# When two expert weight parts are loaded: tables moved in on-chip memory, and the load order of the mixture-of-experts stage's first slots

## The chip, the cores and the metric

The kernel runs on one core of a Trainium2 chip. Times are device microseconds of one launch. The kernel before took 649.22 us, the median of three runs (646.59, 649.22, 649.32).

## The reference, cut to what matters

One step of a one-layer decoder on 544 tokens (512 of a prompt, 32 of 8 samples), width 1024, all in float32:

```
xn     = rms_norm(x); u, v, xr, g_a, g_b = split(xn @ w_in)        # 1024 x 5120
merged = sigmoid(g_a) * (gelu(u) * spatial_gating(layer_norm(gelu(v)))) + sigmoid(g_b) * rg_lru(conv(xr))
x1     = x + merged @ w_out                                         # 1024 x 1024
xf     = rms_norm(x1)
group  = argmax(xf @ w_rg + b_rg)          # of 4; softmax value pg
e1, e2 = top2 of the group's 8 experts     # softmax values pe, renormalised
y      = sum over e1, e2 of gate * ((silu(xf @ w_gate[e]) * (xf @ w_up[e])) @ w_down[e])
out    = rms_norm(x1 + y)
```

There are 32 experts, each with 3 MB of weights (`w_gate`, `w_up` 1024 x 256, `w_down` 256 x 1024), so that about 100 MB must come from memory whatever the tokens choose.

## The kernel before, in words

The first part (to about 300 us of the span) normalises the tokens and computes the input projection, the spatial gating and the recurrent branch, channel block by channel block. The output projection follows: 16 units (numbers 40 to 55, `STEPS` is 56), eight for token group A (tiles 0, 1 and the samples' tile 4), eight for group B (tiles 2, 3). Each unit's weights go through one of four `raw` buffers. Beside the units of group B, VectorE already routes group A. When the last unit is done (`unit_done` = `STEPS`), group B is routed: a rank of every token within its expert, then one-hot tables `posh`, `toks` and `rsk`, from which TensorE makes two tables, first the token indices (`idx`, released by `tab_ready`), then the row scales `rt` (released by `rt_mm`).

The expert stage handles experts in pairs, 64 tokens each, side by side on the 128 partitions. There are 16 pairs and, with these inputs, one further single expert that has more than 64 tokens. For each pair GpSimd gathers 128 token rows from the buffer `xnd` in device memory into `xg` (semaphore `xg_in`), TensorE transposes them (L1817), multiplies by gate and up weights (L1829), transposes the product (L1842), multiplies by the down weights (L1855), and GpSimd scatters the rows to `ytok`. At the end the rows come back (`gy`), are weighted, added to the residual and normalised.

Weights live in six slots of 24 KB a partition, `wslot[q][s]` with q = 0, 1, 2 and s = 0, 1; pair G uses q = G mod 3. Each expert comes in three parts of 1 MB: part 0 (first half of gate and up), part 1 (second half), part 2 (down). All of them are issued by SyncE, in program order, in one queue. SyncE's program around the change: the units' loads `step_in(n)`; experts 0 and 1 have long been in slots (0,0) and (0,1); the loop over n = 48 to 55 also issues the three parts of expert 4 into slot (2,0); then `row_out(p, count)` writes the finished residual tiles to `xnd`, each waiting for VectorE's `x1_ready`; then comes the wait for the last unit, the rest of the six slots, and `refill` for all later pairs, which waits for TensorE to be done with a part (`gu_half`, `gu_mm`, `pair_mm`) before it issues the next one into it.

On-chip memory is laid out by hand, and the six slots overlap with things of the earlier stages. Slot (2,1) covers 72 to 96 KB, of which 72 to 80 KB is the projection's third split buffer, and the rest was free early. Slot (1,1) covers 122 to 146 KB, of which the last 16 KB is `raw`; the routing tables (`R_T`) stood at 138 KB, in its part 2. `dgs` (two diagonal matrices of gates) is made by VectorE after `rt` and announced by `dgs_ready`.

The semaphore names of the prediction: `dgs_ready` (L1336), `rt_mm` (L1790), `xg_in` (L635), `tab_ready` (L1321), `x1_ready` (L1143). SyncE's lines: L467 issues a part of an expert in the opening, L489 a unit, L500 a residual tile, L537 and L553 a refill, L570 the last pair's parts, L581 the final reads.

Of the kernel before, what the change touches and what calls it, by code (L numbers as in the profile page):

```python
# [22 lines left out]
P = 128  # L23
D = 1024
# [4 lines left out]
S = DB * DS  # L29
TA = SEQ + S  # L30
TILES = NT + 1
# [21 lines left out]
GROUP_A, GROUP_B = (0, 3), (3, 5)  # L53
# [55 lines left out]
def build(nc, x, wmix, wgate, chan, wst, bs, rows, wr, br, wmoe, y, vp, vs, st):  # L109
# [3 lines left out]
    def at(name, offset, shape, dt=F32):  # L113
        return nc.alloc_sbuf_tensor_at(name, shape, dt, offset=BASE + offset)

    K = 1024
# [2 lines left out]
    GU = KT * 512  # L119
    EW = GU + 2 * D  # L120
    wslot = [[at(f"wslot{q}{s}", (first + s * 24) * K, [P, EW]) for s in range(2)]
             for q, first in enumerate((0, 98, 48))]
    xh = at("xh", 48 * K, [P, KT, SEQ], F32R)
    xl = at("xl", 64 * K, [P, KT, SEQ], F32R)
    zT = at("zT", 80 * K, [P, KT, TA])

    R_V = 162 * K
    v = at("v", 0, [P, TILES, D])
    x1 = at("x1", R_V, [P, TILES, D])
    tw = TA * 4  # L130
    XRW = 3 + SEQ + DB * 7
    (XC, A, TR, TI, M, U, U1, GA) = [at(n, R_V + i * tw, [P, TA]) for i, n in
                                     enumerate(("xc", "a", "tr", "ti", "m", "u", "u1", "ga"))]
    XR = at("xr", R_V + 8 * tw, [P, XRW])

    R_M = 98 * K
    mh = at("mh", R_M, [P, KT, SEQ], F32R)
    ml = at("ml", R_M + 16 * K, [P, KT, SEQ], F32R)
    xt = at("xt", R_M, [P, TILES, D])
    lng = at("lng", R_M + 20 * K, [P, D])  # L140
    lnb = at("lnb", R_M + 24 * K, [P, D])
    g1r = at("g1r", 80 * K, [P, D])
    junk = at("junk", R_M + 28 * K, [P, D])
    bterm = at("bterm", R_M + 28 * K, [P, KT, P])
    vo = at("vo", R_M, [P, 2, D])

    R_W = 130 * K
    raw = at("raw", R_W, [P, RAW, KT, P])
    wh = at("wh", R_W + 16 * K, [P, 2, D], F32R)
    wl = at("wl", R_W + 24 * K, [P, 2, D], F32R)  # L150

    wh2 = at("wh2", 72 * K, [P, D], F32R)
    wl2 = at("wl2", 76 * K, [P, D], F32R)
    R_T = R_W + 8 * K
    posh = at("posh", R_T, [P, 2, TILES, P], BF16)
    colh = at("colh", R_T + 2560, [P, 2, TILES, PAIRS], BF16)
    toks = at("toks", R_T + 2880, [P, 2, 2, TILES, 2, PAIRS], BF16)
    pick = at("pick", R_T + 4160, [P, 2, TILES, NE])
    rsk = at("rsk", R_T + 5440, [P, 3, 2, TILES, PAIRS], BF16)
    junk2 = at("junk2", 96 * K, [P, 512])  # L160
    yf = at("yf", 122 * K, [P, TILES, D])

    gy = at("gy", 48 * K, [P, 2, TILES, D])
    nf = at("nf", 88 * K, [P, D])
# [1 line left out]

    R_E = R_W + 16 * K
    xg = at("xg", R_E, [P, D])
# [3 lines left out]
    hm = at("hm", R_E + 13 * K, [P, FE])  # L172
    hT = at("hT", R_E + 14 * K, [P, 2, P])

    top = [182 * K]

    def small(name, shape, dt=F32):
        size = 4
        for n in shape[1:]:
            size *= n  # L180
        t = at(name, top[0], shape, dt)
        top[0] += -(-size // 32) * 32
        return t
# [1 line left out]
    ch = small("ch", [P, KT, NCH])  # L185
    ident = small("ident", [P, P])
    ones = small("ones", [P, P], F32)
    upper_at = top[0]
    upper = small("upper", [P, P], F32)
    fold = small("fold", [P, S])  # L190
    late = top[0]
# [47 lines left out]
    first = small("first", [P, NE])  # L239
# [3 lines left out]
    gate = small("gate", [P, 2, TILES])  # L243
    T2 = 2 * TILES
    rk = small("rk", [P, 2, TILES])
    (rkx, chk, bx, posx) = [at(n, upper_at + 256 + i * 64, [P, T2]) for i, n in enumerate(("rkx", "chk", "bx", "posx"))]
    caps = small("caps", [P, MAXCHUNK - 1])
    xcnt = small("xcnt", [P, 3, NE])
    cnt17 = small("cnt17", [1, EXTRA])
# [9 lines left out]
    warm = small("warm", [P, 1])  # L259
    turn = small("turn", [P, 4])  # L260
    eps = small("eps", [P, 1])
    dgs = at("dgs", upper_at, [S, 2, S])
    WH, WL = (wh[:, 0, :], wh[:, 1, :], wh2[:]), (wl[:, 0, :], wl[:, 1, :], wl2[:])
    assert BASE + top[0] <= nc.sbuf_usable_end, top[0] / K

    with ExitStack() as ctx:
        ps = ctx.enter_context(nc.psum_tensor("ps", [P, 8, 512], F32))

        def sem(name):
            return ctx.enter_context(nc.semaphore(name))  # L270
# [13 lines left out]
        xg_in = sem("xg_in")  # L284
# [95 lines left out]
        dgs_ready = sem("dgs_ready")  # L380
# [6 lines left out]
        def rowsof(t):  # L387
            return S if t == NT else P
# [38 lines left out]
        def _(sp_):  # L427
            e = sp_
# [30 lines left out]
            def expert(q, s, n):  # L459

                for part in range(3):
                    expert_part(q, s, n, part)

            def expert_part(q, s, n, part):

                lo, hi = PARTS[part]
                e.dma_start(wslot[q][s][:, lo:hi], wmoe[n][:, lo:hi]).then_inc(part_in[part][q][s], 16)  # L467
# [16 lines left out]
            def step_in(n):  # L484

                e.wait_ge(lo_ready, n - 3)
                if n < O_FIRST + UNITS_O + RAW:
                    e.wait_ge(rows_mm, UNITS_V // 2 + (1, 1, 2, 3, 2, 3, 4, 4)[n - O_FIRST - RAW])
                e.dma_start(raw[:, n % RAW, :, :], wmix[unit_at(n)]).then_inc(raw_in[n % RAW], 16)  # L489
# [6 lines left out]
            def row_out(p, count):  # L496

                t = TILE_AT[p]
                e.wait_ge(x1_ready, count)
                e.dma_start(xnd[t * P:t * P + rowsof(t), :], x1[0:rowsof(t), t, :]).then_inc(xn_stored, 16)  # L500
# [9 lines left out]
                residual_in(p)  # L510
            for n in range(48, STEPS):
                step_in(n)
                if n % 2 and n < 54:
                    expert_part(2, 0, 4, (n - 49) // 2)
            expert_part(2, 1, 5, 1)
            expert_part(2, 1, 5, 2)
            for p in range(*GROUP_A):
                row_out(p, 4 + p)
            row_out(3, 9)
            row_out(4, 10)  # L520
            e.wait_ge(unit_done, STEPS)
            expert(1, 0, 2)
            expert_part(1, 1, 3, 0)
            e.wait_ge(dgs_ready, 2)
            expert_part(1, 1, 3, 1)
            e.wait_ge(rt_mm, 1)
            expert_part(1, 1, 3, 2)
            expert_part(2, 1, 5, 0)

            def refill(q, count, number):  # L530

# [944 lines left out]
        def _(pe):  # L1476
# [48 lines left out]
            def nothing(*_):  # L1525
                pass
# [444 lines left out]
```

## Time and profile before

| | us |
|---|---|
| median of three runs | 649.22 |
| the profiled execution | 649.22 |
| its span in the profile | 647.5 |
| TensorE busy | 599.0 |
| VectorE busy | 322.7 |
| ScalarE busy | 229.3 |
| GpSimd busy | 52.4 |

The span is the time from the first to the last recorded instruction; 1.7 us of the execution lie outside it. The mean of TensorE's granted clock was 0.97 of full speed. All parts of the expert weights, 97 transfers of 1024 KB and four of 512 KB, are issued by SyncE; the page's line of GB/s shows how the transfers are spread over the span. A matmul here streams 512 columns of float32.

### The profile page before, as it was taken

How to read it: one execution, taken by the hardware profiler on the slowest of the kernel's cores; microseconds unless marked ns; L12 is line 12 of the kernel's file. 1: busy time of each engine (PE TensorE's matmuls, PEld its weight loads, DVE VectorE, ACT ScalarE, POOL GpSimd, SP SyncE). 2: the span in 40 equal slices, each digit the busy share in tenths (PEclk: the TensorE clock that was granted, in tenths of full speed). 3: DMA queues.
4: the chain of work that ended last, by engine and by line, in shares of the span. 5: the costliest groups of instructions: out<-in, count | busy, mean ns of one | idle time of the engine just before them, and what ended most of it. 6: DMA issues, size and time to landing. Idle time of an engine off the chain costs nothing.

```text
span 647.5 us, 8845 instructions
## 1 busy us (share of the span) xinstructions
PE 599.0 (93%) x2860; PEld 359.8 (56%) x2860; DVE 322.7 (50%) x672; ACT 229.3 (35%) x393; POOL 52.4 (8%) x126
## 2 busy tenths in 40 slices
PE   6899999999999999999999978999999988987794
PEld 3676697877778777787578733433333333332320
DVE  4834698857767677685664855111001102100058
ACT  5423425474564745647263311111111111111124
POOL 1200001000000000000000021112121221111000
PEclk9899999999999999999997969999999999999996
DMA  8421316731222312222596389999999999999993
GB/s 308 163 86 66 126 37 240 329 106 65 73 73 97 105 65 73 73 98 71 200 412 274 134 325 414 417 420 420 419 420 421 421 419 420 420 418 419 416 320 138
DMA packets 33448, 160.61 MB, mean 248 GB/s; under 512 B 6320, under 2 KB 6704, under 8 KB 21008
## 3 DMA queue, kind: packets, MB, share of 16 engines
q1 hardware_dynamic: 27808, 149.52, 58.6%
q0 software_dynamic: 5472, 10.63, 4.5%
q8 instruction: 14, 0.23, 0.1%
q10 hardware_dynamic: 144, 0.15, 0.1%
q14 instruction: 10, 0.08, 0.0%
HBM read 155.01 MB, written 14.17 MB: 261 GB/s over the span
## 4 chain that ended last, share of the span: by engine, by line
PE 65%; SPq 12%; DMA 9%; DVE 8%; ACT 3%; issue 2%; ACTq 0%; DVEq 0%; POOLq 0%
PE ps L1486 14%; PE ps L1487 13%; PE ps L1488 13%; SPq L537 11%; PE ps L1829 8%; DMA wslot<-in_wmoe 5%; PE ps L1855 5%; PE ps L1605 2%; PE ps L1637 2%; DMA gy<-ytok 2%; PE ps L1691 1%; DMA ytok<-yo,idx 1%; PE ps L1589 1%; PE ps L1495 1%; PE ps L1628 1%
## 5 line engine op out<-in xcount | busy, mean ns | idle before, releaser
L1829 PE MATMUL ps<-wslot,xgT 128*64 128x512 f32 x528 | 121.7, 594 | 11.6 <-DMA wslot<-in_wmoe 10.2
L699 ACT ACTIVATE wh<-raw 128x1024 fp32r<-128x1024 f32 x56 | 59.1, 1058 | 153.5 <-PE ps L1488 138.1
L1486 PE MATMUL ps<-xh,wh 128*128 128x512 f32 x256 | 102.5, 401 | 0.0
L1488 PE MATMUL ps<-xl,wh 128*128 128x512 f32 x256 | 100.0, 390 | 0.0
L1487 PE MATMUL ps<-xh,wl 128*128 128x512 f32 x256 | 99.9, 390 | 0.0
L908 DVE TENSOR_TENSOR wl<-raw,wh 128x1024 fp32r<-128x1024 f32 x56 | 68.5, 1223 | 45.9 <-ACT wh L699 44.9
L1829 PEld LDWEIGHTS ps<-wslot,xgT 128*64 128x64 f32 x528 | 40.0, 137 | 88.5 <-issue 86.6
L1855 PE MATMUL ps<-wslot,hT 128*64 128x512 f32 x264 | 62.1, 599 | 8.2 <-ACT hT L869 8.2
L1402 DVE SCALAR_TENSOR_TENSOR hm<-ps,rt,hs 128x256 f32<-128x256 f32 x12 | 5.8, 484 | 120.6 <-ACT hs L867 120.6
L1486 PEld LDWEIGHTS ps<-xh,wh 128*128 128x128 f32 x256 | 48.1, 188 | 16.1 <-issue 6.7
L1488 PEld LDWEIGHTS ps<-xl,wh 128*128 128x128 f32 x256 | 48.1, 188 | 10.5
L1487 PEld LDWEIGHTS ps<-xh,wl 128*128 128x128 f32 x256 | 48.2, 188 | 9.3
L1855 PEld LDWEIGHTS ps<-wslot,hT 128*64 128x64 f32 x264 | 18.5, 137 | 40.9 <-issue 28.7
L872 ACT ACTIVATE yo<-ps 128x1024 f32<-128x1024 f32 x17 | 17.4, 1023 | 65.4 <-PE ps L1855 65.4
L867 ACT ACTIVATE hs<-ps,rt 128x256 f32<-128x256 f32 x12 | 5.7, 474 | 82.0 <-PE ps L1829 82.0
L1402 DVE SCALAR_TENSOR_TENSOR hm<-ps,rtx,hs 128x256 f32<-128x256 f32 x5 | 2.4, 484 | 57.8 <-ACT hs L867 57.8
L1486 PE MATMUL ps<-wh,xh 128*128 128x512 f32 x64 | 26.8, 418 | 3.1 <-DVE xs L934 2.1
L1486 PE MATMUL ps<-wh,mh 128*128 128x512 f32 x64 | 27.2, 425 | 0.0
L1488 PE MATMUL ps<-wl,xh 128*128 128x512 f32 x64 | 25.9, 405 | 0.0
L1487 PE MATMUL ps<-wh,xl 128*128 128x512 f32 x64 | 25.9, 405 | 0.0
L1487 PE MATMUL ps<-wh,ml 128*128 128x512 f32 x64 | 25.9, 405 | 0.0
L1488 PE MATMUL ps<-wl,mh 128*128 128x512 f32 x64 | 25.8, 402 | 0.0
(331 smaller groups left out, 798.6 us busy)
## 6 DMA issues: line engine op xcount, KB each, us to landing
wslot<-in_wmoe SPq DMA_DIRECT2D x97, 1024.0 KB, 22.2
raw<-in_wmix SPq DMA_DIRECT2D x56, 512.0 KB, 4.1
gy<-ytok SPq DMA_DIRECT2D x8, 512.0 KB, 8.7
xt<-in_x SPq DMA_DIRECT2D x4, 512.0 KB, 7.0
x<-in_x SPq DMA_DIRECT2D x4, 512.0 KB, 4.5
xnd<-x SPq DMA_DIRECT2D x4, 512.0 KB, 8.0
wslot<-in_wmoe SPq DMA_DIRECT2D x4, 512.0 KB, 27.0
out_y<-yf SPq DMA_DIRECT2D x4, 512.0 KB, 2.7
```

The costliest lines, as they stand in the source:

```text
L537: e.dma_start(wslot[q][s][:, lo:hi], wmoe[bass.ds(number + s, 1), :, lo:hi].rearrange("a p c -> (a p) c")).then_inc(part_in[part][q][s], 16)
L699: a.activation(WH[hslot], raw[:, slot, :, :].rearrange("p k c -> p (k c)"), ACT.Copy).then_inc(hi_ready, 1)
L872: a.activation(yo[:], ps[:, 6:8, :].rearrange("p b c -> p (b c)"), ACT.Copy).then_inc(yo_sb, 1)
L908: d.tensor_tensor(WL[hslot], raw[:, slot, :, :].rearrange("p k c -> p (k c)"), WH[hslot].bitcast(F32), ALU.subtract).then_inc(lo_ready, 1)
L1402: d.scalar_tensor_tensor(out=hm[:], in0=ps[:, 2, FE:2 * FE], scalar=scale, in1=hs[:], op0=ALU.mult, op1=ALU.mult).then_inc(hm_ready, 1)
L1486: pe.matmul(out, sh, mh_, start=start, stop=False)
L1487: pe.matmul(out, sl, mh_, start=False, stop=False)
L1488: return pe.matmul(out, sh, ml_, start=False, stop=stop)
L1605: i = pe.matmul(ps[S * q:S * q + S, 6, :].rearrange("p (u c) -> p u c", u=4), xs[:, k, :], raw[:, :, k, :], start=k < 4, stop=k >= 4, tile ...
L1637: pe.matmul(ps[:, 4 + w, :], gw[:, w, :], XC[:, 0:SEQ], start=True, stop=True)
L1829: l = pe.matmul(ps[CAP * s:CAP * s + CAP, 2, :], xgT[:, c, CAP * s:CAP * s + CAP], wslot[q][s][:, c * 512:(c + 1) * 512], start=c == 0, st ...
L1855: l = pe.matmul(ps[CAP * s:CAP * s + CAP, 6 + h, :], hT[:, f, CAP * s:CAP * s + CAP], wslot[q][s][:, o:o + 512], start=f == 0, stop=f == 1 ...
```

## The change

Everything from 98 KB to 182 KB moves down by 1 KB, so that the small tiles have 1 KB more; `rkx`, `chk`, `bx`, `posx` and `dgs`, which shared the bytes of `upper`, get bytes of their own. The routing tables (`R_T`) move from 138 KB to 80 KB, and the scratch tile `junk2` from 96 KB to 88 KB: both now lie in parts 1 and 2 of slot (2,1), and part 2 of slot (1,1) is clear of them. SyncE's order follows:

- Parts 1 and 2 of slot (2,1) (expert 5) are no longer issued ahead of the residual tiles but, with part 0, after the wait for `rt_mm`.
- The wait for `dgs_ready` in front of part 1 of slot (1,1) (expert 3) becomes a wait for the first gather, `xg_in` at 16; part 2 of that slot follows at once and no longer stands behind `rt_mm`.
- The residual tiles of group A are issued inside the loop, after the last unit's load; their order to it is as before.

```diff
     wslot = [[at(f"wslot{q}{s}", (first + s * 24) * K, [P, EW]) for s in range(2)]
-             for q, first in enumerate((0, 98, 48))]
+             for q, first in enumerate((0, 97, 48))]
...
-    R_V = 162 * K
+    R_V = 161 * K
...
-    R_M = 98 * K
+    R_M = 97 * K
...
-    R_W = 130 * K
+    R_W = 129 * K
...
-    R_T = R_W + 8 * K
+    R_T = 80 * K
...
-    junk2 = at("junk2", 96 * K, [P, 512])
-    yf = at("yf", 122 * K, [P, TILES, D])
+    junk2 = at("junk2", R_T + 8 * K, [P, 512])
+    yf = at("yf", 121 * K, [P, TILES, D])
...
-    top = [182 * K]
+    top = [181 * K]
...
-    (rkx, chk, bx, posx) = [at(n, upper_at + 256 + i * 64, [P, T2]) for i, n in enumerate(("rkx", "chk", "bx", "posx"))]
+    (rkx, chk, bx, posx) = [small(n, [P, T2]) for n in ("rkx", "chk", "bx", "posx")]
...
-    dgs = at("dgs", upper_at, [S, 2, S])
+    dgs = small("dgs", [S, 2, S])
...
             for n in range(48, STEPS):
                 step_in(n)
-                if n % 2 and n < 54:
-                    expert_part(2, 0, 4, (n - 49) // 2)
-            expert_part(2, 1, 5, 1)
-            expert_part(2, 1, 5, 2)
-            for p in range(*GROUP_A):
-                row_out(p, 4 + p)
+                if n % 2:
+                    if n < 54:
+                        expert_part(2, 0, 4, (n - 49) // 2)
+                    else:
+                        for p in range(*GROUP_A):
+                            row_out(p, 4 + p)
             row_out(3, 9)
             row_out(4, 10)
             e.wait_ge(unit_done, STEPS)
             expert(1, 0, 2)
             expert_part(1, 1, 3, 0)
-            e.wait_ge(dgs_ready, 2)
+            e.wait_ge(xg_in, 16)
             expert_part(1, 1, 3, 1)
+            expert_part(1, 1, 3, 2)
             e.wait_ge(rt_mm, 1)
-            expert_part(1, 1, 3, 2)
-            expert_part(2, 1, 5, 0)
+            expert(2, 1, 5)
```

## Rows read from the trace of the kernel before

**Rows 1.** the page: GB/s in 40 slices; chain by engine; DMA issues
```profile
GB/s 308 163 86 66 126 37 240 329 106 65 73 73 97 105 65 73 73 98 71 200 412 274 134 325 414 417 420 420 419 420 421 421 419 420 420 418 419 416 320 138
...
PE 65%; SPq 12%; DMA 9%; DVE 8%; ACT 3%; issue 2%; ACTq 0%; DVEq 0%; POOLq 0%
...
wslot<-in_wmoe SPq DMA_DIRECT2D x97, 1024.0 KB, 22.2
```

**Rows 2.** windows of the expert stage: busy us per engine, PEclk, DMA share, GB/s
```profile
384.00:396.00 12.00, 10.06 (x49) 4.58 (x47) 9.34 (x28) 0.47 (x1) 1.49 (x3) 0.92 0.98 384
392.00:480.00 88.00, 81.60 (x438) 31.16 (x436) 16.34 (x32) 12.69 (x26) 16.42 (x26) 1.00 1.02 418
480.00:595.00 115.00, 101.92 (x468) 38.36 (x464) 16.32 (x28) 16.99 (x34) 20.56 (x34) 1.00 1.02 420
```

**Rows 3.** timeline of TensorE, experts' gate/up matmuls: start, us, what, [idle before]
```profile
505.36 7.04 PE L1829 MATMUL ps<-wslot,xgT 128*64 128x512 f32 x32
...
518.08 7.04 PE L1829 MATMUL ps<-wslot,xgT 128*64 128x512 f32 x32
...
532.88 3.65 PE L1829 MATMUL ps<-wslot,xgT 128*64 128x512 f32 x16 [1.86 <-DMA wslot<-in_wmoe]
...
548.84 7.08 PE L1829 MATMUL ps<-wslot,xgT 128*64 128x512 f32 x16
...
589.92 3.65 PE L1829 MATMUL ps<-wslot,xgT 128*64 128x512 f32 x16 [1.40 <-DMA wslot<-in_wmoe]
595.69 3.65 PE L1829 MATMUL ps<-wslot,xgT 128*64 128x512 f32 x16 [2.11 <-DMA wslot<-in_wmoe]
```

**Rows 4.** chain of waits at the end: start us, us, what
```profile
564.90 30.65 DMA wslot<-in_wmoe
...
607.23 8.14 DMA ytok<-yo,idx
```

**Rows 5.** timeline of SyncE's queue: start us, us, what it issued
```profile
337.96 0.91 SPq L467 DMA_DIRECT2D wslot<-in_wmoe  x2
338.92 26.76 SPq L500 DMA_DIRECT2D xnd<-x  x4
...
367.11 3.06 SPq L467 DMA_DIRECT2D wslot<-in_wmoe  x4
...
383.23 1.28 SPq L467 DMA_DIRECT2D wslot<-in_wmoe  x3
...
391.29 0.88 SPq L537 DMA_DIRECT2D wslot<-in_wmoe  x2
```

**Rows 6.** windows around the output projection's second half
```profile
338.00:350.00 12.00, 12.00 (x73) 10.06 (x73) 2.58 (x9) 2.93 (x5) 0.00 (x0) 0.72 1.02 414
351.00:366.00 15.00, 15.00 (x80) 12.71 (x80) 12.66 (x42) 4.55 (x8) 0.00 (x0) 1.00 0.01 4
```

**Rows 7.** what SyncE's queue waited for: us, times, longest
```profile
SPq L467 <- DVE dgs L1336: 13.0, 1, 13.0
```

**Rows 8.** timeline of all engines, gather, tables and gates
```profile
378.67 1.10 POOL L632 DMA_INDIRECT xg<-xnd,idx  x1 [109.30 <-DVE idx L1320]
...
379.11 1.38 PE L1788 MATMUL ps<-rsk,posh 128*128 128x16 bf16 x30
...
382.83 0.37 DVE L1336 TENSOR_SCALAR dgs<-ident,gate 32x32 f32<-32x32 f32 x2
383.47 0.18 PEld L1817 LDWEIGHTS ps<-ident,xg 128*128 128x128 f32 x1 [0.80 <-DMA xg<-xnd,idx]
```

**Rows 9.** windows of the gap before the stream
```profile
379.50:383.00 3.50, 3.50 (x32) 2.06 (x32) 1.30 (x9) 0.20 (x1) 1.30 (x2) 0.50 0.59 194
383.00:384.00 1.00, 1.00 (x2) 0.18 (x1) 0.21 (x2) 0.00 (x0) 0.00 (x0) 0.50 0.05 21
```

**Rows 10.** timeline of TensorE, the second and third pair
```profile
401.46 7.04 PE L1829 MATMUL ps<-wslot,xgT 128*64 128x512 f32 x32
...
416.27 4.08 PE L1829 MATMUL ps<-wslot,xgT 128*64 128x512 f32 x18
```

More of the change, by code:

```diff
@@ L187, in build @@
     ones = small("ones", [P, P], F32)
-    upper_at = top[0]
     upper = small("upper", [P, P], F32)
```

## The prediction

> **What bounds the kernel now.** The page comes first. Its line of GB/s shows two kinds of stretches: loads well under 330 through most of the first half, then a plateau of 414 to 421 from slice 25 to slice 38, that is from about 389 us to 615 us [rows 1]. The chain that ended last puts 65% on TensorE and 12% and 9% on SyncE's queue and on transfers [rows 1], but these are shares of the whole span, and the plateau has to be read by itself. The windows of that stage show the 16 DMA engines busy all the time (share 1.02) at 418 and 420 GB/s, with TensorE busy for 81.6 of 88 us and for 101.9 of 115 us [rows 2]. So transfers run flat out from the start of the stage; TensorE is served from filled slots at first and has caught up with the loads later. The timeline shows when: up to 518.08 us the pairs follow each other every 12.72 us without a wait; from 532.88 us on, gate and up matmuls begin after waits on `wslot` (1.86, 1.40 and 2.11 us in the three rows that show one, of five in all) [rows 3]. The last such wait sets the end. The chain goes through a weight transfer to 595.55 us (564.90 + 30.65), then one pair's matmuls, its scatter (8.14 us) and the final reads behind that [rows 4]. After 595.55 us, 51.95 us remain to the end of the span at 647.5 us, and nothing in them is touched by the change.
>
> The end is thus the start of the stream, plus all bytes that must follow, over 420 GB/s, plus a fixed tail. What counts about a part is whether it goes before the stream's start, in time in which the DMA engines have nothing else to do, or into the stream.
>
> **Two parts lose their free place.** Before, parts 1 and 2 of slot (2,1) are issued at 337.96 us, ahead of the residual tiles [rows 5]. The DMA engines are then busy until about 350 us (share 1.02), and idle for the 15 us from 351 to 366 us, at 4 GB/s [rows 6]. The two parts cost nothing there: without them the same stretch is idle for 20 us. After, they stand behind `rt_mm`, in the stream. Each is 1024 KB [rows 1], both are 2.10 MB, and at the 420 GB/s of rows 2 they take 4.99 us. The bounds are 4.9 us by 430 GB/s, a little over the plateau's fastest slice, and 5.5 us by the 384 GB/s of the stream's first 12 us, where it is still starting [rows 2]. I take 5.0, since the queue is never empty later, so that the bytes are paid for at the plateau's rate.
>
> The Trainium skill's "DMA: Bandwidth & Descriptors", section "Where 436 GB/s comes from", says that for loads from device memory the memory's side binds, at about 358 GB/s. By it the two parts would cost 5.9 us (an estimate from that page's figure) and the time would be 655.3 us. The plateau of 420 GB/s on this core disagrees, and the measurement decides.
>
> **The stream's restart.** Four parts are issued at 367.11 us in both kernels [rows 5]. Then SyncE waits. Before, it waits 13.0 us for `dgs` [rows 7] and issues the next three parts at 383.23 us [rows 5], just after VectorE's two `dgs` operations end at 383.20 [rows 8]. After, it waits for the first gather. GpSimd issues that at 378.67 us, once the index table is there, and TensorE, which waits for the same semaphore `xg_in`, begins to load the first gathered rows at 383.47 us, after 0.80 us of idle time put down to that gather [rows 8]. So `dgs_ready` goes and `xg_in` is late next, 0.2 us later: I take a restart at 383.45. Its early bound is the end of the gather's issue, 379.77 us, a gain of 3.5 us (nothing excludes that the semaphore came before TensorE looked); its late bound is 384.2, a cost of 1.0. For the value near `xg_in` = 383.4 speaks the window ahead of it: 194 GB/s of gather and scatter traffic from 379.5 to 383 us and only 21 in the next [rows 9], which is how the end of a gather and a scatter looks.
>
> Behind the new wait stand five parts and then every refill; nothing else is in SyncE's queue until the end. The `rt_mm` wait behind it costs nothing: that matmul group ends at 380.49 us (379.11 + 1.38) [rows 8], before the gather lands. Issuing goes at 0.43 us each (three in 1.28 us), so the five are out by 385.6 us, ahead of the first refill, which TensorE releases at 391.29 us [rows 5].
>
> **What depends on the delayed parts.** Parts 1 and 2 of slot (1,1) land some 5 us after the restart, at 389 us; the second pair needs them at 401.46 us. Slot (2,1), three parts, follows by about 396 to 398 us (5.24 MB at 420 GB/s from 383.5, plus gather traffic); the third pair needs them at 416.27 us [rows 10]. Both are covered, with 12 and 18 us to spare, so no pair stalls early. The refills queue behind 2.1 MB more and land 5 us later each; up to the eleventh pair this only eats the lead of the filled slots.
>
> **Edits without a cost.** The addresses change no instruction: the same forms on other offsets; `rkx` to `dgs` only get bytes of their own. If offsets mattered to VectorE's speed, its few dozen small operations of 0.2 us could shift by tenths of a microsecond; below that I have no row, and take 0 (from -0.2 to +0.2). The residual tiles of group A go out 0.9 us earlier (337.96 rather than 338.92 [rows 5]) and land about 5 us earlier, with the 2 MB gone from in front. Nobody waits for them: the first gather had been waiting for the index table [rows 8], and the last tile goes out in both cases just before 367.11. Gain 0.
>
> **Sum.** Profiled execution 649.22 us (span 647.5, 1.72 around it, and equal to the median shown). 649.22 + 4.99 + 0.22 = 654.4 us.
>
> **Rivals.** *TensorE's chain sets the end and the transfers are hidden.* For it: TensorE is busy for 93% of 392 to 480 us. Its point of decision is whether the weights' landings still have 5 us to spare at the last pairs. Then only the restart of the loads moves, nobody waits for it, and the time stays at 649.2 to 649.4 us, not slower. Against it: the waits of rows 3, from 532 us on, the last of them on the chain. Chance 0.08.
>
> *The gather lands well before TensorE looks.* The stream then restarts 2 to 3.5 us earlier, and the time is 650.9 to 652.4 us, middle 651.7. For it: TensorE was in filler matmuls around 383 us. Against it: the traffic of rows 9. Chance 0.09.
>
> *The projection gets its clock back.* Over 338 to 350 us TensorE's granted clock was 0.72 in the mean, while the DMA engines were saturated, and 1.00 from 351 to 366 us, when they were idle [rows 6]. If the 2 MB of traffic are the cause, 12 us at 0.72 shrink by 3.4, and everything behind comes as much earlier: 651.0 us. Against it: the router's short matmuls stand in this stretch, and the same DMA share beside the experts' matmuls goes with a clock of 1.00 [rows 2]. Chance 0.04.
>
> *Longer waits cost the clock.* With the loads 5 us later TensorE waits in more pairs. If a wait took it down to the 1.2 GHz level, the 7.3 us of matmuls of the chain after the last landing (3.65 of gate and up [rows 3], and as many of the same width for down) would double: 654.4 + 7.3 = 661.7 us. Against it: granted clock 1.00 over 480 to 595 us with waits of up to 2.11 us [rows 2, 3]. For it: 0.50 from 379.5 to 384 us, after a stretch of small matmuls and gaps [rows 9]. Chance 0.04. The Trainium skill's "TensorE: Matmul & The Clock Gate", section "HAM oscillation — how this bites in real kernels", says that a wait for a transfer between groups of matmuls sends the array back to its slow clock, group after group. By that rule the time is this rival's; the 1.00 in rows with such waits does not bear it out so far.
>
> **From the cases to the numbers.** The forecast has 0.75, and its own range is 653.2 to 655.8 us. The rest is 0.08, 0.09, 0.04, 0.04. Below 0.5% (3.2 us, the least that a measurement of this kernel can tell from no change) lie the first rival and most of the second and third, 0.08 + 0.07 + 0.03 = 0.18; one of the three runs before was 2.6 us below the others, so 0.02 of it goes to faster and 0.02 more of the forecast's goes to the same. That makes faster 0.02, same 0.18, slower 0.80. The range runs from 651.2 to 656.4: it takes in both ends of the transfer's price, the late restart, and the upper part of the early ones.
>
> **What would show it.** In the profile after: no weight parts between 338 and 366 us, and an idle DMA stretch of about 20 us that begins near 345. SyncE's wait ahead of L467 put down to the gather's `xg`, ending 0.2 us behind where the `dgs` wait ended, then five parts in a row. The pairs start at the same times up to about 500 us, with no wait at the second and third pair. The share stays at 1.02 and the rate at 420 GB/s. A pair takes 15.96 us once TensorE has caught up (from 532.88 to 548.84) against 12.72 before [rows 3], a loss of 3.2 us each, so its first wait on `wslot` comes one or two pairs earlier, around 505 to 520 us. The last landing in the chain moves from 595.5 to about 600.8 us, with the same 52 us behind it. The prediction falls if that landing moves by less than 2 us, if the restart is not at 383.2 to 384 us, or if a pair before the tenth waits for its weights.

## The result, and the profile after

The changed kernel takes 653.44 us, the median of nine runs, against 649.01 us of nine runs of the kernel before beside it. The ratio is 1.0066 (95% interval 1.0048 to 1.0085), that is 3.1 to 5.5 us slower. One of the nine took 865.06 us, in a slow state with a granted clock of 0.65 in the mean, and the ratio leaves it out. A second set of six runs gave 653.43 against 648.56 us and a ratio of 1.0070 (1.0050 to 1.0091). The ratios and their intervals are estimates from single runs and need not be the quotient of two medians. The profiled execution took 652.5 us, its span 650.9 us; before it was 649.22 and 647.5.

The page of the changed kernel, with the same two lines as in [rows 1]:

```profile
GB/s 309 159 87 66 128 34 257 310 106 73 68 68 97 105 73 73 64 107 86 217 407 103 220 331 421 419 420 419 417 422 420 420 419 421 419 419 420 413 315 137
...
PE 62%; SPq 16%; DMA 9%; DVE 8%; ACT 3%; issue 2%; ACTq 0%; DVEq 0%; POOLq 0%
```

In slices 21 to 23 (325 to 374 us) 407, 103 and 220 GB/s stand where the kernel before has 412, 274 and 134. Traffic is gone from slice 22, in the idle stretch, and the later stages' plateau of 413 to 422 runs as before. The windows that answer to [rows 2, 6] (columns as there):

```profile
338.00:350.00 12.00, 12.00 (x81) 10.16 (x80) 3.98 (x18) 2.93 (x5) 0.00 (x0) 0.86 0.70 254
392.00:480.00 88.00, 81.67 (x438) 31.42 (x438) 14.16 (x24) 13.81 (x28) 15.86 (x27) 1.00 1.02 420
480.00:595.00 115.00, 98.59 (x450) 37.73 (x448) 16.31 (x28) 15.88 (x32) 20.30 (x33) 1.00 1.02 420
```

The share stays 1.02 and the rate 420 GB/s. TensorE is busy for 98.6 us instead of 101.9 between 480 and 595 us, so it waits more. SyncE's queue, as in [rows 5]:

```profile
337.82 1.38 SPq L499 DMA_DIRECT2D xnd<-x  x3
...
365.33 3.06 SPq L466 DMA_DIRECT2D wslot<-in_wmoe  x4
...
381.57 2.58 SPq L466 DMA_DIRECT2D wslot<-in_wmoe  x5
...
388.95 4.26 SPq L536 DMA_DIRECT2D wslot<-in_wmoe  x4
```

The residual tiles come at 337.82 us with nothing in front of them, and the five parts in a row at 381.57 us. What the queue waited for there, as in [rows 7], and then the gather's issue and the `dgs` operations, as in [rows 8]:

```profile
SPq L466 <- DMA xg<-xnd,idx: 13.2, 1, 13.2
```

```profile
376.85 1.10 POOL L631 DMA_INDIRECT xg<-xnd,idx  x1 [107.63 <-DVE idx L1319]
...
379.94 0.38 DVE L1335 TENSOR_SCALAR dgs<-ident,gate 32x32 f32<-32x32 f32 x2
```

Here `dgs` was there at 380.32 us (379.94 + 0.38), 1.25 us ahead of the gather, while before the two were 0.2 us apart. The first wait of TensorE for weights, which before came at 532.88 us [rows 3]:

```profile
508.56 3.65 PE L1828 MATMUL ps<-wslot,xgT 128*64 128x512 f32 x16 [1.94 <-DMA wslot<-in_wmoe]
```

Over the whole stage these waits in front of the gate and up matmuls, in us, times and longest, were in the kernel before and then in the changed one:

```profile
PE ps L1829 <- DMA wslot<-in_wmoe: 10.2, 7, 2.1
```

```profile
PE ps L1828 <- DMA wslot<-in_wmoe: 14.6, 10, 2.1
```

And the chain at the end, as in [rows 4]:

```profile
567.96 30.67 DMA wslot<-in_wmoe
...
598.76 3.67 PE ps L1828 x16
...
610.31 8.04 DMA ytok<-yo,idx
```

The last landing of the chain moved from 595.55 to 598.63 us (567.96 + 30.67), by 3.08. That is less than the forecast's 5.2. The difference of the two profiles divides as follows, with the first of the four parts at `unit_done` as a mark (367.11 before, 365.33 after):

| us | before | after | difference |
|---|---|---|---|
| until the first of the four parts | 367.11 | 365.33 | -1.78 |
| from there to the restart | 16.12 | 16.24 | +0.12 |
| from the restart to the last landing in the chain | 212.32 | 217.06 | +4.74 |
| from there to the end of the span | 51.95 | 52.27 | +0.32 |
| span | 647.5 | 650.9 | +3.4 |

The third line is the two parts' price. Between these two marks 88.32 MB flow in the kernel before, at 416 GB/s in the mean, and 90.47 MB in the changed one, at 417. The first line was not in the forecast's sum, and had to be explained.

### The profile page after: what moved, and what is told of

Same layout as the page of the kernel before. It is cut to its first block, busy times and chain, and to the rows that moved or that the text cites. A ratio compares the mean times of both kernels' runs of the same rounds, so it can differ in the third digit from the quotient of the medians.

```text
span 650.9 us, 8845 instructions
## 1 busy us (share of the span) xinstructions
PE 597.5 (92%) x2860; PEld 357.2 (55%) x2860; DVE 322.5 (50%) x672; ACT 229.0 (35%) x393; POOL 51.7 (8%) x126
## 4 chain that ended last, share of the span: by engine, by line
PE 62%; SPq 16%; DMA 9%; DVE 8%; ACT 3%; issue 2%; ACTq 0%; DVEq 0%; POOLq 0%
SPq L536 14%; PE ps L1485 14%; PE ps L1487 13%; PE ps L1486 13%; PE ps L1828 6%; DMA wslot<-in_wmoe 5%; PE ps L1854 4%; PE ps L1604 2%; PE ps L1636 2%; DMA gy<-ytok 2%; DMA ytok<-yo,idx 1%; PE ps L1690 1%; PE ps L1588 1%; PE ps L1494 1%; PE ps L1627 1%
## 5 line engine op out<-in xcount | busy, mean ns | idle before, releaser
L1828 PE MATMUL ps<-wslot,xgT 128*64 128x512 f32 x528 | 122.1, 594 | 16.1 <-DMA wslot<-in_wmoe 14.6
L1487 PEld LDWEIGHTS ps<-xl,wh 128*128 128x128 f32 x256 | 48.0, 188 | 10.6
```

Of the source, the lines that this page charges most:

```text
L1487: return pe.matmul(out, sh, ml_, start=False, stop=stop)
L1828: l = pe.matmul(ps[CAP * s:CAP * s + CAP, 2, :], xgT[:, c, CAP * s:CAP * s + CAP], wslot[q][s][:, c * 512:(c + 1) * 512], start=c == 0, st ...
```

## The experiments

All ratios are to the kernel before, run beside it on the same chip. For each profile the table has TensorE's granted clock in 338 to 350 us, the issue of the first of the four parts (A), the restart (R) and the last landing in the chain (L), read as in the rows above.

| kernel | ratio(s) | clock | A | R | L - R |
|---|---|---|---|---|---|
| before | 1 | 0.72 | 367.11 | 383.23 | 212.32 |
| changed | 1.0066, 1.0070 | 0.86, 1.00 | 365.33, 364.51 | 381.57, 380.55 | 217.06, 217.11 |
| before, both parts late | 1.0053, 1.0079 | 0.86, 0.72 | 365.70, 367.44 | 380.86, 383.52 | 217.52, 216.97 |
| changed, `dgs` wait | 1.0037, 1.0075 | 0.72, 1.00 | 367.53, 364.15 | 382.71, 380.21 | 216.86, 217.11 |
| before, gather wait | 0.9992 | 0.86 | 366.00 | 381.83 | 213.85 |
| before, one part late | 1.0028 | 0.72 | 367.21 | 383.33 | 214.54 |
| changed, four parts late | 1.0138 | 0.72 | 367.85 | 383.13 | 221.94 |
| before, TensorE delayed | 1.0113 | 0.72 | 367.78 | 383.92 | 219.60 |
| changed, TensorE delayed | 1.0106 | 0.72 | 367.33 | 383.51 | 219.11 |

Two kernels below have no line, one for want of a restart, the other for want of such a last landing: the one without the pause (clock 0.86, A 365.89) and the one with lighter refills (0.72, 368.22).

### Both parts late, and nothing else

```diff
-            expert_part(2, 1, 5, 1)
-            expert_part(2, 1, 5, 2)
...
-            expert_part(2, 1, 5, 0)
+            expert(2, 1, 5)
```

> The kernel before with one edit: the two early parts (1 and 2 of slot (2,1)) are issued where the change has them, with part 0, behind the wait for rt_mm. Addresses and the wait for dgs_ready stay. Stream theory (the end is restart + bytes / 420 GB/s + a fixed tail): from the restart (the issue behind the wait) to the last weight landing of the chain 217 us instead of 212.3, and the time 4.7 to 5.0 us above before, or less by what the projection's low-clock stretch gives back. Rival 'the clock is given back by the missing 2 MB': granted clock in 340 to 350 us 0.83 as in the changed kernel (0.66 before), the last unit done 1.7 us earlier, time +3.1 to 3.3. Rival 'that was chance': over the rounds, the mean clock is that of before, and the time is +4.7 to 5.0.

652.82 us against 649.36, ratio 1.0053 (1.0034 to 1.0072). In the profile the stretch R to L is 217.52 us: this edit alone has the whole price of the change. The clock of 340 to 350 us was 0.83 and the time 3.5 us above before, nearer to the rival of the clock (3.1 to 3.3) than to the 4.7 to 5.0 without it. The second run of this kernel, below, has the other clock.

### The gather wait, and nothing else

```diff
-            e.wait_ge(dgs_ready, 2)
+            e.wait_ge(xg_in, 16)
```

> The kernel before with one edit: SyncE waits for the first gather (xg_in) instead of dgs_ready before part 1 of slot (1,1). Both parts stay early. Stream theory: the restart moves from 16.1 us to 16.2 us behind the first of the four parts' issue, time +0.1 to +0.3 us. In the changed kernel's trace dgs_ready would have been there 1.2 us ahead of the gather, so at most +1.2 us. Rival 'the gather wait is the cost of the change': +3 us or more. No clock change expected in 340 to 350 us, since the 2 MB stay.

648.99 us against 649.36, ratio 0.9992 (0.9974 to 1.0010): the new wait costs nothing that can be measured. Its profile shows two further things. First, the granted clock (the third column from the right) and, at 402 us, a hole in the stream:

```profile
338.00:350.00 12.00, 12.00 (x81) 10.06 (x80) 4.00 (x16) 2.93 (x5) 0.00 (x0) 0.86 1.01 408
402.00:404.00 2.00, 2.00 (x12) 0.65 (x10) 0.00 (x0) 0.83 (x2) 0.18 (x1) 1.00 0.59 139
```

Secondly, what made the hole. The first pair's down matmuls, 3.65 us long in the kernel before, took 5.35 us, because TensorE's granted clock was at its lower level (0.50, that is 1.2 GHz) for some 3.4 us of them, from about 397.4 to 400.8 us:

```profile
396.32 5.35 PE L1855 MATMUL ps<-wslot,hT 128*64 128x512 f32 x16 [0.47 <-ACT hT L869]
```

```profile
397.83:399.83 2.00, 2.00 (x8) 0.73 (x6) 0.00 (x0) 0.00 (x0) 0.00 (x0) 0.50 0.98 406
```

The release of part 2 of the first slot came 1.7 us later for it, and SyncE's next issue at 401.91 us. The queue had all but run out by then, and two microseconds passed at 139 GB/s. R to L is 213.85 us, 1.5 more than before.

### The changed kernel with the dgs wait

```diff
-            e.wait_ge(xg_in, 16)
+            e.wait_ge(dgs_ready, 2)
```

> The changed kernel with one edit back: dgs_ready instead of xg_in before part 1 of slot (1,1). It differs from the parts-late kernel only by the addresses and by the place of part 2 of slot (1,1) against rt_mm. Stream theory: the changed kernel's time less 0.1 to 1.2 us, that is +2 to +4.3 us over before; and equal within 0.5 us to the parts-late kernel, because addresses cost nothing. Rival 'the addresses matter' (slower small operations or transfers): over 1 us away from the parts-late kernel.

651.43 us against 649.36, ratio 1.0037 (1.0018 to 1.0056), lower than its sibling with the old addresses; the profile has 216.86 us from R to L, 0.7 less. The medians of the two are 1.4 us apart, where I had expected 0.5 at most and had set over 1 us as the sign that the addresses matter. So it was run again, below.

### Four parts late

```diff
-                        expert_part(2, 0, 4, (n - 49) // 2)
+                        if n == 49:
+                            expert_part(2, 0, 4, 0)
...
+            expert_part(2, 0, 4, 1)
+            expert_part(2, 0, 4, 2)
             expert(2, 1, 5)
```

> The changed kernel with the dose doubled: parts 1 and 2 of slot (2,0) (expert 4) also go behind rt_mm, so 4 MB instead of 2 MB are missing from the idle stretch. Stream theory: another 5.0 us over the changed kernel (about +8 to +9.5 us over before), 222 us from restart to the last landing of the chain. Rival 'TensorE hides the rest' (only part of a delayed MB reaches the end): less than +3 us over the changed kernel. Rival 'the clock is given back by the missing traffic': the granted clock in 338 to 350 us rises further, towards 1.00, and the last unit is done earlier again.

658.56 us, ratio 1.0138 (1.0117 to 1.0158), 9.2 us over before. The chain's weight transfer ends at 605.07 us, 221.94 us behind the restart, so the second pair of parts costs 4.8 us like the first:

```profile
574.39 30.68 DMA wslot<-in_wmoe
```

The clock in 338 to 350 us is 0.72, the lowest of the three values seen, although all but the units' loads, one part and the tiles are gone from there. The rival that blamed the traffic expected it to rise.

### No pause ahead of the stream

```diff
-            e.wait_ge(dgs_ready, 2)
             expert_part(1, 1, 3, 1)
+            expert_part(2, 1, 5, 0)
             e.wait_ge(rt_mm, 1)
             expert_part(1, 1, 3, 2)
-            expert_part(2, 1, 5, 0)
```

> The kernel before without the pause: SyncE does not wait for dgs_ready; behind the four parts at unit_done it issues part 1 of slot (1,1) and part 0 of slot (2,1) at once, and part 2 of slot (1,1) behind rt_mm, so that the 2 MB come some 4 us earlier. Plain stream theory of the prediction (end = restart + bytes / 420 + tail): 2.5 to 3.5 us faster than before, 646 us. Rival 'thin queue' (before, the preload is through at 391.3 us, just when TensorE releases the first part for a refill, and nearly through again at 401.9 us, so an earlier restart only makes an idle stretch ahead of that release): no gain, -0.5 to +0.5 us, and +1 to +3 if the first gather, now beside weight traffic, lands later and with it the first release. In the profile: GB/s well below 420 for some us ahead of the first refill.

654.67 us against 648.89, ratio 1.0087 (1.0057 to 1.0116): my plain sum would have had this kernel 3 us faster, and it is 5.8 us slower, more than the rival's 1 to 3 us as well. TensorE waits for the first gather to 385.7 us, and then has its first gate and up matmuls at half clock for a part of their 9.65 us (7.09 before):

```profile
385.74 1.97 PE L1816 MATMUL ps<-ident,xg 128*128 128x128 f32 x8 [2.71 <-DMA xg<-xnd,idx]
389.12 9.65 PE L1828 MATMUL ps<-wslot,xgT 128*64 128x512 f32 x32 [1.42 <-DVE xgT L1382]
```

Meanwhile the preloaded slots are full, and there is nothing to load before TensorE's first release at 395.6 us. Nine microseconds at 57 GB/s:

```profile
387.00:396.00 9.00, 7.58 (x24) 2.37 (x24) 7.58 (x23) 0.00 (x0) 1.24 (x2) 0.59 0.17 57
```

In the kernel before the first gate and up matmuls begin at 387.36 us and the first release is at 391.29. Here they begin 1.8 us later, behind the gather, and last 2.6 us longer by the clock, which makes the release 4.3 us later. From that release to the last landing in the chain it is 204.1 us here (395.62 to 599.73) and 204.3 in the kernel before (391.29 to 595.55): with the queue dry, the release is the start that counts.

### TensorE delayed, in both kernels

```diff
                 pe.wait_ge(yo_sb, FIRST + G)
+                if isinstance(G, int) and G == 0:
+                    keep_warm(8, 6, ident)
```

> The kernel before, with eight filler matmuls of 512 columns (about 3.7 us) in front of the first pair's down matmuls, so that TensorE releases part 2 of that slot, and everything behind, 3.7 us later. Plain stream theory: no change, since TensorE has about 140 us to make up for it (-0.3 to +0.3). Thin-queue theory: the queue runs dry at 402 us until the release, +2.5 to +3.7 us, and a stretch of low GB/s there.

> The same eight filler matmuls in the changed kernel. Plain stream theory: no change over the changed kernel. Thin-queue theory: the 2 MB more that stand in the queue cover 4.8 us, so again no change or at most +0.7 us; the two delayed kernels then differ by only 1 to 2.5 us, where the undelayed ones differ by 3.3 to 4.3 us. If the delayed kernels differ by 4 us or more, the thin-queue theory is wrong.

656.30 us and 656.08 us against 648.89; ratios 1.0113 (1.0089 to 1.0136) and 1.0106 (1.0080 to 1.0131). The filler was longer than I had meant: eight matmuls show as 16 and take 7.1 us in the profile of the changed kernel, and 8.8 us in that of the one before, where the granted clock was at 0.50 for 3.4 us of it:

```profile
397.31 8.83 PE L1482 MATMUL ps<-ident 128*128 128x512 f32 x16 [0.47 <-ACT hT L869]
```

In the kernel before the queue is dry at about 404.6 us and stays so until SyncE's next issue at 409.96:

```profile
406.00:409.00 3.00, 3.00 (x15) 1.06 (x16) 0.00 (x0) 0.00 (x0) 0.00 (x0) 1.00 0.00 0
```

In the changed kernel it is dry from about 408.5 us, and the next issue is at 408.96; the two worst microseconds:

```profile
408.50:410.50 2.00, 2.00 (x12) 0.72 (x10) 0.00 (x0) 1.11 (x2) 0.18 (x1) 1.00 0.44 82
```

The queue lasts 20.7 us from the restart in the one (383.92 to 404.6) and 25.0 us in the other (383.51 to 408.5). The delay costs 7.4 us in the kernel before, and some 2.5 us in the changed one, by the ratios (1.0106 against 1.0068 in the mean of its two undelayed sets). In the profiles L - R grows by 7.3 and by 2.0 us, and 1.7 of the 7.3 belong to the low clock in that one execution. All of this is more than the 2.5 to 3.7 and 0 to 0.7 us that I had expected of a filler of 3.7 us. The delayed kernels are equal within their intervals, although one has its two parts early; I had expected 1 to 2.5 us between them, and 4 us or more would have spoken against the thin queue.

### Lighter refills

```diff
                 for part, used in enumerate((gu_half, gu_mm, pair_mm)):
                     lo, hi = PARTS[part]
...
+                    hi = lo + 64 if part == 2 else hi
```

> The kernel before with less data to load: each refill's part 2 (down weights) loads only its first 64 of 2048 columns, about 24 MB less; everything else runs as before on what the slots hold. It shows how far TensorE's own chain lies below the end. Stream theory: TensorE never waits for weights, pairs of 12.7 us throughout, so the end comes 8 to 10 us earlier (639 to 641 us). Rival 'TensorE's chain sets the end and loads are hidden': within 1 us of before.

This kernel leaves most of the down weights out, and the experts compute with what the slots still hold. It takes 633.82 us, ratio 0.9767 (0.9742 to 0.9792). TensorE's own chain ends 15 us below the kernel's time; I had expected 8 to 10. It never waits for weights, and the rate falls to 360 GB/s:

```profile
480.00:580.00 100.00, 94.61 (x438) 35.41 (x434) 15.18 (x28) 15.54 (x31) 18.21 (x30) 1.00 0.94 360
```

### Half the dose, and three kernels again

```diff
-            expert_part(2, 1, 5, 2)
...
             expert_part(2, 1, 5, 0)
+            expert_part(2, 1, 5, 2)
```

> Half the dose: the kernel before with only part 2 of slot (2,1) moved behind rt_mm; part 1 stays early. Straight price (4.8 us for 2 MB from the first MB on): +2.4 us. Thin-queue theory (before, TensorE's first release comes 2 us ahead of the dry queue at best, and a run in which it is later loses DMA time; the first MB late fills just that): less than half, +0.7 to +1.8 us.

> The parts-late kernel once more, beside the two others on one chip. Addresses cost nothing: within 1 us of the changed kernel with the dgs wait. Straight price of 2 MB: +4.8 us over before; with the dry stretches of before counted, +3 to +4.

> The changed kernel with the dgs wait once more. If its +2.4 us was the spread of runs, it is now +3 to +4 us over before, within 1 us of the parts-late kernel; if the addresses gain something, it stays 1.5 us below it.

> The changed kernel once more on this chip: +3.5 to +4.5 us over before. Against the same kernel with the dgs wait it shows what the gather wait costs: 0 to +1 us, since in the profiles the gather came 0.6 to 1.1 us later behind the first four parts than dgs.

One part late: 650.42 us against 648.56, ratio 1.0028 (1.0011 to 1.0044), 1.8 us; L - R is 2.2 us longer. That is the upper end of the thin queue's 0.7 to 1.8 us and below the straight price of 2.4, and its interval holds both. The others: 654.81, 653.37 and 653.43 us, ratios 1.0079, 1.0075 and 1.0070, each within 0.0021. So the low value of the changed kernel with the `dgs` wait was the spread of runs. Neither the addresses nor the choice of the wait makes a difference that can be measured, though by the medians the kernel with the old addresses was 1.4 us above its sibling both times, so that an effect of the addresses below some 1 us is not excluded. The mean of the six ratios with two parts late is 1.0063, 4.1 us.

The second run with both parts late happens to test the thin queue once more. In its profile the first pair's down matmuls take 5.35 us too, again with the clock at 0.50:

```profile
396.99 5.35 PE L1853 MATMUL ps<-wslot,hT 128*64 128x512 f32 x16 [0.47 <-ACT hT L867]
```

```profile
399.00:400.00 1.00, 1.00 (x4) 0.24 (x2) 0.00 (x0) 0.00 (x0) 0.00 (x0) 0.50 1.07 434
```

SyncE's next issue is as late, at 402.58 us: 12.3 us behind the first refill in both, where the kernel before has 10.6. But the queue with the two late parts in it lasts: 401 GB/s from 400 to 402 us and 420 from 402 to 404, and L - R is 216.97 us like its siblings.

Two of the last profiles settle the line of the table that I had not forecast. The window of 338 to 350 us in the changed kernel with the `dgs` wait (second run):

```profile
338.00:350.00 12.00, 12.00 (x88) 10.12 (x87) 5.56 (x19) 3.48 (x6) 0.00 (x0) 1.00 0.71 285
```

Clock 1.00, and the four parts go out at 364.15 us. In all fourteen profiles the clock has one of three values there, and A follows it: 0.72 with 367.1 to 368.2 us, 0.86 with 365.3 to 366.0, 1.00 with 364.2 to 364.5. A clock of 0.86 is one stretch of 3.4 us at 0.50 within the 12 us, 0.72 one of 6.8 us, as in the kernel before:

```profile
342.00:348.00 6.00, 6.00 (x19) 5.03 (x20) 0.15 (x1) 0.00 (x0) 0.00 (x0) 0.50 1.01 410
```

With the 2 MB in place it was 0.72 three times and 0.86 twice; without them 0.72 four times, 0.86 twice and 1.00 twice; with one of the two parts 0.72. The traffic alone does not set the clock. Whether its absence makes 1.00 more likely can't be said from so few profiles.

## Why the prediction was right, and where it was off

- **The plateau is the bound: right.** 420 GB/s at share 1.02 in both kernels, 14.6 us of waits for weights in the gate and up matmuls where the kernel before has 10.2, and TensorE's chain 15 us below the end in the kernel with lighter refills. The rival in which TensorE hides the rest is out. Two readings ahead of it were wrong without harm: the kernel before has seven waits for weights and not five (two more, at 606.40 and 611.37 us, belong to the single expert, behind the wait of 595.69 us, and are not on the chain), and the 15.96 us of a pair that has caught up was one interval only; the mean of the four from 532.88 to 589.92 us is 14.3.
- **Two parts lose their free place, 4.99 us: right in kind, a little too large.** The stretch from the restart to the last landing grows by 4.5 to 5.2 us in six profiles (mean 4.8), all against the one value of 212.32 us before, and by another 4.8 for two more parts. The bytes are there about as forecast, 2.15 MB more between the marks, but the mean rate rises from 416 to 417 GB/s with them, which is worth 0.4 us. With the parts late alone the whole price is there.
- **The restart, +0.22 us: right from mark to mark.** It is +0.12 us in the pair of profiles. In absolute time it came at 381.57 us, outside the 383.2 to 384 that were given as a sign of being wrong, and the last landing at 598.63 instead of 600.8, both because everything from the first of the four parts on came 1.78 us earlier. The forecast's sum had no term for that. In the changed kernel `dgs` would have been there 1.25 us ahead of the gather, so the forecast's 0.2 was the accident of one profile; yet the runs show no cost of the gather wait. The rival in which the gather lands well before TensorE looks (0.09) is out: SyncE goes on 4.7 us behind the gather's issue (376.85 to 381.57), and in the kernel before TensorE began 4.8 us behind it.
- **Dependants are covered, addresses and tiles cost nothing: right.** The second and third pair did not wait; the ratios of the three kernels with old and new addresses agree within 0.1% in the last set, which leaves room for less than about 1 us.
- **The first wait for weights: 505 to 520 us was forecast, 508.56 measured.**
- **"The queue is never empty later": wrong for the kernel before.** This is the only step that the runs contradict, and it can account for a part of the 1 us by which the forecast was too slow (5.2 against 4.1 us in the mean of six ratios, 4.4 us in the first medians). After the restart the kernel before has 3 MB in hand, and its refills wait for TensorE's releases at 391.29 and 401.87 us. By the 20.7 us of the delayed kernel its queue lasts until about 403.9 us, two microseconds more. One late release, as in the profile with the gather wait, opens a hole of 1.5 us; the same late release opens none in the profile with both parts late. The two late parts cost 4.8 us of transfer but also fill the queue up to 25 us, so that the changed kernel has no such hole. The two delayed kernels show this directly. How often the kernel before has a hole in an undisturbed run, and so whether holes explain all of the gap between 4.8 us in profiles and 4.1 us in runs, stays open: the profiled one has none at 402 us. As far as the mean clock of a span shows it, the clock does not explain the gap. Over all runs on record the kernel before takes 648.96 us in the mean (52 runs, mean granted clock 0.976) and the kernels with both parts late 652.97 us (62 runs, 0.975), 4.0 us more at a clock that is no higher.
- **The rival in which the projection gets its clock back (0.04): not borne out.** The profiled pair looks like it, 1.78 us earlier at the first mark. But 0.72 and 0.86 both occur with and without the 2 MB, and the difference belongs to the spread of runs as far as these profiles show.
- **The rival in which longer waits cost the clock (0.04, 7.3 us): not borne out in its size, but it happens.** In the profiled pair the clock stays at 1.00 behind every wait for weights, up to 2.12 us. Over all the profiles there are fourteen such waits of 2.08 to 2.30 us; behind ten of them the clock stayed at 1.00, behind four it fell to 0.50 for 3.4 us, which costs 1.7 us and not 7.3. The forecast had nothing for it. The page that the prediction cites here (the Trainium skill's "TensorE: Matmul & The Clock Gate", section "HAM oscillation — how this bites in real kernels") tells of waits of about 3 to 5 us, longer than any of these.

The plain sum would have failed on another change: taking out the pause looks like 3 us won and loses 5.8.

## What to carry to other kernels

When transfers run flat out to the end, a transfer moved from idle time into the stream costs its bytes over the plateau's rate, whatever is hidden behind it; read the rate from the windows and the idle time ahead of the stream before moving anything. But a stream fed by freed slots has a second start, the first release by the engine that uses them: an earlier restart gains nothing if the queue only runs dry ahead of that release, and it loses if the first gather has to share the engines, so that the release comes later (here 1.8 us by the gather and 2.6 us by the clock). Compare marks within each profile (an issue, a restart, a last landing) rather than ends of spans: the clock's chance moved the ends by 1.8 us, while the stretch between two marks repeated within 0.7 us over six profiles. Where one group of equal matmuls is longer than its siblings, look at the granted clock in a window of its own before looking for a wait.

## What the runs showed that I had not expected

TensorE's clock in one 12 us stretch of the projection takes one of three mean values from run to run (0.72, 0.86, 1.00: two, one or no times 3.4 us at 0.50) and moves the issue of the four parts by 1.6 us a step. The three levels span 3.3 to 4 us, about the spread of runs of one kernel.

The same happens, more rarely, in the expert stage. In six of the fourteen profiles one or two groups of 16 matmuls take 1.7 us longer than their siblings, seven in all: at 396.32 and 396.99 us (both shown above), in the filler at 397.31 (8.83 us instead of 7.13), at 514.97, 598.52 and 602.76 us, and here at 600.62 us in the second run with both parts late:

```profile
600.62 5.35 PE L1827 MATMUL ps<-wslot,xgT 128*64 128x512 f32 x16 [2.08 <-DMA wslot<-in_wmoe]
```

In each of them the granted clock is 0.50 for 3.4 us (here from 601.9 to 605.3 us) and 1.00 on either side. Four follow a wait of 2.08 to 2.30 us for weights, by 0.5 to 1.3 us. The three near 397 us follow the first pair's short transposes with waits of 0.47 to 1.59 us between them, which other profiles have too without a fall. Why the clock falls in one execution and not in the next is not shown.

Behind the last landing such a stretch goes straight into the end: the three profiles that have it there (both with the parts late, and the changed kernel delayed) show 52.9 to 53.8 us from the last landing to the end of the span, the others 51.9 to 52.5. Ahead of the first refills it can open a hole in a thin queue. In between, at 514.97 us in the kernel with four parts late, TensorE's loss does not show in L - R.

With weight transfers beside it the first gather took 8.3 us from its issue to TensorE's use (377.45 to 385.74 us, in the kernel without the pause) and 4.8 us without them (378.67 to 383.47 us [rows 8]).
